# Tiles of the full and of the local attention in turns, instead of one kind after the other

## What is computed

```python
SEQ = 512; CTX_LEN = 256; DEPTH = 2; HEAD_DIM = 64; WINDOW = 128; Q_BLOCK = 128

def global_block_attention(q, k, v, k_c, v_c):        # full: 4 query heads, 2 key heads
    ...
        s_lat = jnp.einsum('bqgrd,bkgd->bgrqk', qi, k, ...) * scale
        s_ctx = jnp.einsum('bqgrd,bcgd->bgrqc', qi, k_c, ...) * scale
        w = jax.nn.softmax(jnp.concatenate([s_lat, s_ctx], axis=-1), axis=-1)
    ...
def window_block_attention(q, k, v, k_c, v_c, sink):   # local: a window of latent keys, all context keys, a sink
    ...
    ok = ((jnp.abs(qpos[:, :, None] - kpos[:, None, :]) <= WINDOW) & ...)
    ...
    w = jax.nn.softmax(jnp.concatenate([s_win, s_ctx, s_sink], axis=-1), axis=-1)
    ...
```

## Time and profile before

| | us |
|---|---|
| median of 3 runs | 1770.73 (1767.09 to 1772.96) |
| the profiled execution, its own time | 1768.33 |
| its span | 1766.5 |
| PE busy | 1673.9, 95% of the span |
| DVE busy | 1165.0, 66% |
| ACT busy | 861.1, 49% |
| exponentials of attention, layer 0 | first at 307.43, last unit at 406.11 |
| exponentials of attention, layer 1 | first at 1255.24, last unit at 1328.21 |

### The profile page before, as it was taken

How to read it: one execution, slowest core, us unless ns; L and a number is a source line. 1 busy time by engine, 2 the same in 40 slices (tenths; PEclk the granted TensorE clock), 3 DMA queues, 4 the chain that set the end, 5 groups by cost and what they waited for, 6 DMA issues and landing times. The chain is left out here.

```text
span 1766.5 us, 29062 instructions
## 1 busy us (share of the span) xinstructions
PE 1673.9 (95%) x11814; PEld 1483.8 (84%) x11814; DVE 1165.0 (66%) x1580; ACT 861.1 (49%) x1372; POOL 267.4 (15%) x212
## 2 busy tenths in 40 slices
PE   6999999989899999999999989999898989999998
PEld 4779898767778999999999968879677787989897
DVE  5466546666538897886986966754767494747472
ACT  5333325646317664555546573332655284527161
POOL 0233641401110000000000024352311200000000
PEclk8999999999999999999999999999999999999999
DMA  9541113200146548358177024222300346546351
GB/s 386 146 176 49 49 49 108 96 1 2 68 171 230 223 149 319 141 203 312 68 286 267 29 99 137 73 108 82 134 1 1 119 188 242 202 157 251 107 191 48
DMA packets 45457, 250.28 MB, mean 142 GB/s; under 512 B 5998, under 2 KB 7452, under 8 KB 26652
## 3 DMA queue, kind: packets, MB, share of 16 engines
q1 hardware_dynamic: 43420, 245.49, 37.4%
q10 hardware_dynamic: 1920, 3.15, 0.5%
HBM read 218.73 MB, written 26.74 MB: 139 GB/s over the span
## 5 line engine op out<-in xcount | busy, mean ns | idle before, releaser
L888 POOL TENSOR_TENSOR w_lo<-raw,w_hi 128x512 fp32r<-128x512 f32 x124 | 178.9, 1474 | 933.8 <-ACT w_hi L1028 912.1
L3622 PE MATMUL ps<-op_hi,w_hi 128*128 128x384 f32 x880 | 298.3, 339 | 5.8 <-ACT x_add L1616 2.8
L3622 PE MATMUL ps<-op_hi,w_lo 128*128 128x384 f32 x880 | 295.7, 336 | 0.0
L3622 PE MATMUL ps<-op_lo,w_hi 128*128 128x384 f32 x880 | 295.7, 336 | 0.0
L3622 PEld LDWEIGHTS ps<-op_hi,w_hi 128*128 128x128 f32 x880 | 165.4, 188 | 13.0 <-issue 7.4
L3622 PEld LDWEIGHTS ps<-op_lo,w_hi 128*128 128x128 f32 x880 | 165.5, 188 | 0.0
L3622 PEld LDWEIGHTS ps<-op_hi,w_lo 128*128 128x128 f32 x880 | 165.4, 188 | 0.0
L1576 ACT ACTIVATE w_hi<-raw 128x1024 fp32r<-128x1024 f32 x96 | 102.0, 1065 | 125.3 <-PE ps L3622 64.8
L1490 ACT ACTIVATE w_hi<-raw 128x1024 fp32r<-128x1024 f32 x80 | 82.6, 1053 | 135.4 <-PE ps L3585 118.2
L2697 DVE TENSOR_TENSOR w_lo<-raw,w_hi 128x1024 fp32r<-128x1024 f32 x96 | 116.4, 1220 | 22.2 <-ACT w_hi L1576 22.0
L3293 PE MATMUL ps<-w_hi,h_hi 128*128 128x256 f32 x448 | 130.1, 290 | 0.0
(11 more groups left out here) (414 smaller groups left out, 3973.0 us busy)
## 6 DMA issues: line engine op xcount, KB each, us to landing
raw<-w_big SPq DMA_DIRECT2D x96, 1024.0 KB, 6.1
raw_m<-w_modl SPq DMA_DIRECT2D x21, 1024.0 KB, 6.3
op_hi<-op_cache SPq DMA_DIRECT2D x21, 768.0 KB, 4.8
op_lo<-op_cache SPq DMA_DIRECT2D x21, 768.0 KB, 6.5
raw<-w_modl SPq DMA_DIRECT2D x14, 1024.0 KB, 4.9
op_hi<-op_cache SPq DMA_DIRECT2D x21, 512.0 KB, 4.2
op_lo<-op_cache SPq DMA_DIRECT2D x21, 512.0 KB, 6.1
first_mod<-w_modl SPq DMA_DIRECT2D x8, 1024.0 KB, 20.9
```

The costliest lines, as they stand in the source:

```text
L888: ins = nc.gpsimd.tensor_tensor(w_lo[r][:, ks, :], src[:, ks, :], w_hi[r][:, ks, :].bitcast(F32), ALU.subtract)
L3622: ins = mm(bank(base + g, 0, h), wide(w)[:, k, g * P:(g + 1) * P], ops[hl][:, k, 0:h], start=(p in FRESH and k == 0 and q == 0), stop=(k = ...
```

## The change

One line of `att_pairs`: the list of full and the list of local tiles are zipped, so that a full tile and a local tile follow each other.

```diff
     def att_pairs(l):
         js = (range(TILES), (0, 4, 1, 5, 2, 3)) if l == 0 else (range(LAT_TILES), range(LAT_TILES))
-        return [(m, j, p) for m in range(2) for j in js[m] for p in range(2)]
+        return [(m, j, p) for at in zip(*js) for m, j in enumerate(at) for p in range(2)]
```

## The result

The change makes the kernel slower, by 0.8%. The median is 1784.21 us (five runs, 1778.74 to 1787.87) against 1769.78 us for the kernel before beside it (five runs, 1767.09 to 1772.96): a ratio of 1.008, interval 1.0056 to 1.0105. The forecast was 1769.4, within 1764.5 to 1774.5. The profiled execution took 1787.87 us, its span is 1786.0; it is the longest of the five.

The account below looks back on a forecast made before the run. PE's own work was taken to bound full units, a serial score-maximum-exponential chain local ones. Layer 1 -0.9, layer 0 -0.1 + 0.7, clock -1.0 gave -1.3: 1767.0 us profiled, 1769.4 as median, range 1764.5 to 1774.5.

Parts of the forecast that it names:

- the chain A of an E unit: Local attention, 8-block unit: time from the end of its scores until the score banks are free, 3.04 us.
- A of the M unit 7: Local attention, 10-block unit: time from the end of its scores until the score banks are free, 3.43 us.
- The rule for one step: Attention: a step is the larger of PE's other work and the score-to-exponential chain, plus next scores; about 1 us error per layer.
- F units behind a local tile: Full-attention units: the first after a local tile falls to its chain, 4.17 us, from 4.41 or 4.85.
- M units in layer 1: 10-block local units: exponentials stay 4.9 us apart, set by the chain, with PE still idle before the masks.
- Layer 1, -0.9: Layer 1's attention, 13 steps: 60.3 us before, 59.5 after, a gain of 0.9 before rounding.
- Layer 0, -0.1: Layer 0's attention, 21 steps: 85.9 us before, 85.8 after, without the pieces on ACT.
- the sigmoid, +0.7: Layer 0, u = 6: the sigmoid's last piece on ACT delays a context tile's next exponential, costing 0.7 us; bounds 0 and 1.2.
- The clock, -1.0: Layer 0: one PE half-clock dip less, gaining 1.0 us; bounds 2.0 gained and 2.0 lost.
- The slower side: Whole kernel slower by more than 0.3%: chance 0.06, including half of the 0.02 left for the unseen.
- the second rival: Attention: PE's clock dips at swings between full and context or local tiles; with five more, 1778.9 us; chance 0.05.
- the waits of local units would be filled: Attention rival: mixing fills PE's idle 10.4 us in layer 0 and 4.9 in layer 1, giving 1755.4 us; chance 0.09.

Follow-up runs that it names:

- with POOL's reads away: Kernel after, with POOL's last weight split and scan-output products in each attention stage replaced by memsets: 1770.01 us against 1771.85, ratio 0.999.
- both kernels that are rid of the waits: Kernel after with the sink as scalar operand in two small DVE instructions, 1771.31 us; kernel after with POOL reads replaced by memsets, 1770.01 us.
- With scalar operands in both: Kernels before and after, each with the sink as a scalar operand in the two small DVE instructions: 1773.11 us (ratio 1.0011) and 1771.31 us (0.9994).
- turns in layer 1 alone: New alternating tile list in layer 1 only, layer 0 in the order of before: 1777.74 us against 1771.57, ratio 1.0024.

## Why the prediction was wrong

**The step that failed** is the treatment of DVE. The prediction said that the change "removes and adds no instruction", and of DVE only that its pieces at u = 1 and u = 4 "meet F or E units with as much room as before: 0, with 0.2 as the upper bound of each". That is a statement about room on DVE. It leaves out that an instruction's own length can depend on what another engine does at that moment. POOL has 12.6 us of reads at the start of layer 0's stage and 10.2 in layer 1's. Its busy time stood in rows 1 (10.01 us in the stretch of F units), but no term of the sum uses it. In the terms of the sum, what failed is the chain A of an E unit, 3.04 us: it was measured where POOL was idle and was used for unit 2, beside whose small instructions POOL reads. The same holds for A of the M unit 7 in layer 1, and for the 0 of the piece at u = 1 in layer 0 (L2114).

**What it cost.** In layer 0 the three steps from unit 1 to unit 4 took 7.92 + 8.02 + 4.97 = 20.91 us in after and 4.43 + 4.27 + 4.29 = 12.99 with POOL's reads away: 7.9 more. The three waits above hold 5.6 of it (6.10 less 3 times 0.16), and L2114 0.9 (2.68 against 1.75). The last 1.4 lies in steps that are run at 1.2 GHz in part; a stretch of 6.8 us at half the clock can cost 3.4 at most, less where PE idles in it (an estimate from its length). In layer 1 the steps to units 2, 3, 4, 7 and 8 took 6.8 us more (30.52 against 23.72), with 5.4 us of waits in them against 1.6 left in the other kernel, so 3.8 of it are waits. The other 3.0 lie in the steps to units 3 and 4 (6.76 + 6.27 against 4.28 + 4.29 us, less a wait of 1.5), where the stretch of 6.8 us at 1.2 GHz is. So the waits of after are some 11 us together, and most of the rest goes with the clock. No run has the waits without the fall of the clock; in both kernels that are rid of the waits the loss is gone as a whole.

**The rule for one step** held elsewhere. F units behind a local tile were to lie 4.17 apart: in layer 1 after, 4.18 behind the E tile, and 4.38 and 4.24 behind the M tiles. M units in layer 1 were to lie 4.92 apart, and PE idle before the masks. After, layer 1, ACT:

```profile
1318.81 0.80 ACT L1323 ACTIVATE prob<-ps,nb 128x640 f32<-128x640 f32 x1 [2.20 <-DVE se L1955]
...
1323.71 0.79 ACT L1323 ACTIVATE prob<-ps,nb 128x640 f32<-128x640 f32 x1 [1.98 <-DVE se L1955]
```

1323.71 - 1318.81 = 4.90, where the rule has 3.43 + 1.49 = 4.92. PE's idle time there was 0.32 us in place of 0.75, as the fuller steps should have it, with the step no shorter. Mixing does not shorten what the chain sets; that part of the reasoning stands.

**Layer 1, -0.9:** right in sign, less than half in size. With scalar operands in both, 74.25 fell to 72.27, that is 2.0. Which steps give more than the rule has was not worked out.

**Layer 0, -0.1, and the sigmoid, +0.7:** with no waits and no fall of the clock, 97.22 us against 99.62 before, in which three stretches at 1.2 GHz lie. The two in M steps cost some 1.0 each (5.90 and 6.06 us from one unit to the next where the rule has 4.92). The first, from 311.2 on, cost nothing that shows: units 0 to 2 lie 10.04 us apart with it and 10.05 in the kernel with turns in layer 1 alone, which has none there. That leaves 97.5 against 97.22, about no change, where the two terms have +0.6. The 0.7 was too much: the delay of unit 7 is real (0.4) and is made up one step later. The prediction stopped one step too early, and it left out a delay of unit 5 by the first piece (0.6), made up as well.

**The clock, -1.0:** wrong. There were as many stretches at 1.2 GHz in the stages, three, but longer ones: 17.0 us in place of 10.2, the two long ones behind or within PE's long idle times.

**The range.** The bounds that the prediction names for its range add up to 1762.1 to 1777.1 if all fall on one side, and not to 1764.5 to 1774.5. The result lies outside of both.

**The rivals.** The slower side had 0.06. Its mechanism was the clock following the thin steps; the sign came, for another reason. Turns without POOL's reads have no stretch at 1.2 GHz in either stage, so the mixture does not have to bring them. It is not cleared by that one execution: turns with scalar operands have 3.4, 3.4 and 6.8 us of them in layer 0, with no long wait, and the order of before has 10.2 us of them with the tensor operands and 3.4 with the scalar ones. What sets their number from kernel to kernel is open. The page "TensorE: Matmul & The Clock Gate" of the Trainium skill (section "HAM oscillation — how this bites in real kernels"), by which the second rival went, speaks of waits; the long waits here came from POOL. That the waits of local units would be filled did not happen either: the M steps stayed as they were.

**What could have been seen beforehand.** The lines at 1293.59 and 1294.29 of before, 0.66 and 0.96 us for an instruction that takes 0.16 elsewhere, and POOL's train of reads (instructions that follow each other with no gap) over them. With L947 and L950 as long as they are shown above, a bound of one whole wait through each of the two, at unit 2 (an estimate), would have been 2.74 + 3.42 - 0.32 = 5.8 us in layer 0 and 1.90 + 2.34 - 0.32 = 3.9 in layer 1, on the slower side.

## What to carry to other kernels

When a change moves work past other work, lay the timelines of all engines over the new place, also of those that the change does not touch and that are far from being the bound; POOL was busy for 15% of the span. Look for instructions of one shape whose longest duration is several times the median (here 661 and 962 ns against 160), and ask what ran beside the long ones, because in the new order more of them may stand there. For tiny DVE instructions with two SBUF inputs on a critical chain, a scalar operand in place of the second tensor costs 0.05 us each here, and none of them waited for POOL.

## What was not expected of the hardware

That a DVE instruction on one column can wait through a whole train of POOL instructions, 15.51 us for some 15 reads of 1.0 us with hardly a gap between them, and 2.92 us for the three that remained of a train of six. One read of POOL's is thus no upper bound for the wait; with a write between the reads, no wait was longer than 1.09 us.
